# The start of an expert stage: clears and a diagonal moved to other engines, the first gather split in two

## What is computed

```python
h = modulate(rmsnorm(x, norm_g[i, 1]), sh2, sc2)
x = x + g2[:, None, :] * hier_moe(h, ...)        # 32 experts, 2 of them for each token

p_top, g_sel = lax.top_k(p_group, 1)             # one of 4 groups of 8 experts
e_val, e_sel = lax.top_k(fine, TOP_E)            # two experts in the group
gate = p_top * softmax(e_val)
y = (silu(x_rows @ w_gate[e]) * (x_rows @ w_up[e])) @ w_down[e]   # 1024 -> 512 -> 1024
out = zeros.at[row_token].add(y * row_gate)
```

## Time and profile before

| | us |
|---|---|
| median of 3 runs | 2112.96 (2109.74 to 2113.27) |
| the profiled execution | 2108.52 |
| its span in the profile | 2106.8 |
| PE busy | 2007.1 (95%) |
| DVE busy | 907.2 (43%) |
| ACT busy | 364.6 (17%) |
| POOL busy | 90.4 (4%) |
| transfers | 592.65 MB, mean 281 GB/s |

### The profile page before, as it was taken

One profiled execution on the slowest core, in us unless ns is written; L12 is line 12 of the kernel. 1 busy time (PEld: TensorE's weight loads), 2 busy tenths in 40 slices (PEclk: granted clock), 3 DMA queues, 4 the chain that ended last, 5 costly groups with the idle time before them and its releaser, 6 DMA issues.

```text
span 2106.8 us, 21679 instructions
## 1 busy us (share of the span) xinstructions
PE 2007.1 (95%) x8126; PEld 1108.9 (53%) x8126; DVE 907.2 (43%) x1851; ACT 364.6 (17%) x747; POOL 90.4 (4%) x179
## 2 busy tenths in 40 slices
PE   8989999998999999799999999989999999999997
PEld 5556666555766658454444344447765444344442
DVE  3354562335355337776676666752444011000102
ACT  2321000032100010121111111112332111111110
POOL 1121110011111000000000000000000000000000
PEclk9999999999999999999999999999999999999999
DMA  7337885232588641539999999973252999999995
GB/s 274 125 109 255 304 321 202 105 131 109 209 320 301 251 167 40 203 152 406 422 420 427 422 422 420 422 259 120 80 200 81 409 427 423 420 415 421 419 417 222
DMA packets 109524, 592.65 MB, mean 281 GB/s; under 512 B 16663, under 2 KB 21270, under 8 KB 84886
## 3 DMA queue, kind: packets, MB, share of 16 engines
q1 hardware_dynamic: 96406, 541.48, 64.0%
q0 software_dynamic: 13056, 50.33, 6.3%
HBM read 590.74 MB, written 1.05 MB: 281 GB/s over the span
## 4 chain that ended last, share of the span: by engine, by line
PE 89%; DVE 4%; DMA 2%; ACT 2%; issue 1%; POOL 1%; SPq 0%; POOLq 0%; DVEq 0%; ACTq 0%
PE bank L1091 31%; PE bank L752 11%; PE bank L765 10%; PE bank L976 6%; PE bank L688 6%; PE bank L1082 5%; PE bank L1077 5%; PE bank L889 3%; PE bank L996 2%; DMA ring<-in_moe_w_up 2%; PE bank L800 1%; PE bank L1207 1%; ACT work L1571 1%; PE bank L1225 1%; PE bank L1116 1%
## 5 line engine op out<-in xcount | busy, mean ns | idle before, releaser
L1091 PE MATMUL bank<-ring,work 128*64 128x512 f32 x3072 | 677.0, 595 | 29.1 <-ACT work L1571 27.8
L1091 PEld LDWEIGHTS bank<-ring,work 128*64 128x64 f32 x3072 | 229.8, 137 | 444.6 <-issue 444.0
L2378 DVE SCALAR_TENSOR_TENSOR work<-work 128x512 f32<-128x512 f32 x384 | 258.6, 745 | 5.1 <-DVE work L2375 4.9
L752 PE MATMUL bank<-hT,ring 128*128 128x256 f32 x1024 | 223.4, 379 | 0.7 <-ACT hT L1365 0.7
L765 PE MATMUL bank<-ring,work 128*128 128x512 f32 x512 | 222.5, 592 | 0.0
L752 PEld LDWEIGHTS bank<-hT,ring 128*128 128x128 f32 x1024 | 194.4, 190 | 32.6 <-issue 6.9
L2382 DVE SCALAR_TENSOR_TENSOR work<-work,bank 128x512 f32<-128x512 f32 x32 | 22.0, 688 | 428.6 <-ACT work L1559 428.6
L2100 DVE SCALAR_TENSOR_TENSOR work<-ring,cond,work 128x512 f32<-128x512 f32 x168 | 126.3, 752 | 105.6 <-DMA ring<-in_ada_w 100.4
L765 PEld LDWEIGHTS bank<-ring,work 128*128 128x128 f32 x512 | 97.2, 190 | 115.6 <-issue 114.8
L976 PE MATMUL bank<-hT,ring 128*128 128x256 f32 x608 | 137.5, 388 | 0.5 <-ACT hT L1479 0.5
L688 PE MATMUL bank<-ring,hT 128*128 128x512 f32 (+1 forms) x320 | 135.0, 579 | 0.0
(11 more groups left out here) (384 smaller groups left out, 1514.3 us busy)
## 6 DMA issues: line engine op xcount, KB each, us to landing
ring<-in_moe_w_gate SPq DMA_DIRECT2D x64, 2048.0 KB, 13.3
ring<-in_moe_w_up SPq DMA_DIRECT2D x64, 2048.0 KB, 16.4
ring<-in_moe_w_down SPq DMA_DIRECT2D x64, 2048.0 KB, 12.3
ring<-in_ada_w POOLq DMA_DIRECT2D x48, 1024.0 KB, 9.5
ring<-in_w_up SPq DMA_DIRECT2D x16, 2048.0 KB, 13.1
ring<-in_w_down SPq DMA_DIRECT2D x16, 2048.0 KB, 10.0
ring<-in_w_in SPq DMA_DIRECT2D x10, 2048.0 KB, 7.8
ring<-in_cd_w_in SPq DMA_DIRECT2D x6, 2048.0 KB, 9.3
```

What stands on the lines that cost most here:

```text
L752: last = pe.matmul(B(4 + b)[:, (c % 2) * S:(c % 2) * S + S], w[:, k, c * P:c * P + P], hT[:, k, :], start=(k == 0), stop=(k == DT - 1))
L1091: last = pe.matmul(b[h, :], x[:, k, h], w[e][:, k, c0:c0 + 512], start=(k == 0), stop=(k == kk - 1))
L2378: mo.do(dve.scalar_tensor_tensor(fl(bias[:, h]), mask_b, rbt[:, bass.ds(12 * bk + h, 1)], fl(bias[:, h]), ALU.mult, ALU.add))
```

## The change

It does these things at once.

- Entry: POOL clears `zeros`, `pgT` and `ye` behind the root of the second row, and ACT builds `dg_m` behind its copies. DVE copies out its share of the transposed tokens ahead of the second row's squares (`between`). `first_hot` does two dependent operations as one for each row. PE does all four clears before it waits for the selection; the pass count gets a bank and a count of its own.
- The first gather is `gather_pair(0)`, for two experts, 128 columns instead of 256. The other two experts' gather, `gather_pair(1)`, stands between the down halves of the first pair. The first quad is written out for this, and the loop runs over the six in the middle. The counts of `gathered` and `xt_drained` are renumbered (`XT_PASS`).
- In every pair `hidden` waits for the first down half's drain ahead of the gate product, and for the second half's ahead of the up product.
- DVE's bias sums are dealt out anew: a whole bucket ahead of the next `pick`, a whole one behind it, one less after the quad.
- Exit: the first scatter waits for the halves one by one, `updated` works by halves in both rows, and the first row's squares go to ACT (`first_squares`).

The diff, cut to this; indentation is reduced and empty lines are left out:

```diff
@@ -649,6 +650,12 @@
 for n, (cols, width) in enumerate(STATS2):
     power2(n, cols, width)
+    if n in (NORM_STAT[1] + 1, NORM_STAT[3] + 1):
+        own.do(pool.memset(zeros, 0.0))
+        own.do(pool.memset(pgT, 0.0))
+        own.do(pool.memset(ye, 0.0))
+        own.wait()
+        pool.sem_inc(sM["zero_ready"], 1)
...
@@ -1052,13 +1059,14 @@
     pe.wait_ge(m["zero_ready"], i + 1)
     clear((3,))
+    pe.wait_ge(m["exp_in"], 2 * i + 1)
+    clear((0, 1, 2))
     pe.wait_ge(m["sel_ready"], i + 1)
     pe.matmul(B(5)[:, 0:NE], earlier[:, :], sel_e[:, 0, :], start=True, stop=True)
     pe.matmul(B(5)[:, NE:2 * NE], ones[:, :], sel_e[:, 0, :], start=True, stop=False)
-    pe.matmul(B(5)[:, NE:2 * NE], earlier[:, :], sel_e[:, 1, :], start=False, stop=True)
-    pe.matmul(B(5)[:, 2 * NE:3 * NE], ones[:, :], sel_e[:, 0, :], start=True, stop=False)
-    pe.matmul(B(5)[:, 2 * NE:3 * NE], ones[:, :], sel_e[:, 1, :], start=False, stop=True).then_inc(m["rank_ps"], 1)
-    clear((0, 1, 2))
+    pe.matmul(B(5)[:, NE:2 * NE], earlier[:, :], sel_e[:, 1, :], start=False, stop=True).then_inc(m["rank_ps"], 1)
+    pe.matmul(B(4)[:, 0:NE], ones[:, :], sel_e[:, 0, :], start=True, stop=False)
+    pe.matmul(B(4)[:, 0:NE], ones[:, :], sel_e[:, 1, :], start=False, stop=True).then_inc(m["rank_ps"], 1)
...
@@ -1077,11 +1085,24 @@
                 last = pe.matmul(b[:, (d % 2) * S:(d % 2) * S + S], xn[:, t, d * P:d * P + P], pick[:, t, :], start=(t == 0), stop=(t == TT - 1))
         last.then_inc(m["gathered"], 1)
-    def scatter(t, ends=False):
+    def gather_pair(j, xt, banks):
+        for piece, b in enumerate(banks):
+            if piece >= 2 and j == 1:
+                pe.wait_ge(m["xt_drained"], xt + piece - 1)
+            for d in (2 * piece, 2 * piece + 1):
+                for t in range(TT):
+                    last = pe.matmul(b[:, (d % 2) * P:(d % 2) * P + P], xn[:, t, d * P:d * P + P], pick[:, t, P * j:P * j + P],
+                                     start=(t == 0), stop=(t == TT - 1))
+            last.then_inc(m["gathered"], 1)
+    def scatter(t, ends=False, drained=None):
         for hf in range(2):
+            if drained is not None:
+                drained(hf)
...
@@ -1091,17 +1112,17 @@
             last = pe.matmul(b[h, :], x[:, k, h], w[e][:, k, c0:c0 + 512], start=(k == 0), stop=(k == kk - 1))
         return last
-    def hidden(it, j):
+    def hidden(it, j, xt):
         pr = 2 * it + j
         x = xeT[:, :, P * j:P * j + P]
-        pe.wait_ge(m["y_drained"], 2 * pr + 2)
         for b, c, name in ((G, 0, "g_filled"), (U, 1, "u_filled")):
+            pe.wait_ge(m["y_drained"], 2 * pr + 1 + c)
             pe.wait_ge(landedM[c], 16 * pr + 16)
             pe.wait_ge(landedM[c + 3], 16 * pr + 16)
             for k in range(DT):
-                if c == 0 and j == 0 and k % 2 == 0:
-                    pe.wait_ge(m["xt_drained"], 4 * it + 1 + k // 2)
+                if c == 0 and k % 2 == 0:
+                    pe.wait_ge(m["xt_drained"], xt + 1 + k // 2)
                 last = product(b, x, (wslot[c], wslot[c + 3]), k, DT, 0)
             last.then_inc(m[name], 1)
...
@@ -1138,14 +1159,18 @@
                 pe.wait_ge(m["pickg_ready"], it + 1)
             gates_turned(it, j)
             down(pr, 0)
+            if first and j == 0:
+                pe.wait_ge(m["pg_drained"], pr + 2)
+                gather_pair(1, xt + 4, (X, T, X, T))
             if more and j == 1:
+                done = xt + (8 if first else 4)
                 pe.wait_ge(m["p_ready"], it + 2 + i)
                 pe.wait_ge(m["pg_drained"], pr + 2)
                 gather(0, X)
                 gather(1, T)
-                pe.wait_ge(m["xt_drained"], 4 * it + 5)
+                pe.wait_ge(m["xt_drained"], done + 1)
                 gather(2, X)
-                pe.wait_ge(m["xt_drained"], 4 * it + 6)
+                pe.wait_ge(m["xt_drained"], done + 2)
                 gather(3, T)
             down(pr, 1)
...
@@ -1154,14 +1179,14 @@
         pe.wait_ge(m["p_ready"], it0 + 1 + i)
         pe.wait_ge(s2["xn_scaled"], i + 1)
         pe.wait_ge(m["y_drained"], 2 * PAIRS * (q + before) + 2)
-        for piece, b in enumerate((G, U, X, T)):
-            gather(piece, b)
-        with pe.Fori(0, QUADS - 1) as qd:
-            quad((q + before) * QUADS + qd, True)
-        quad((q + before) * QUADS + QUADS - 1, False)
+        xt0 = (q + before) * XT_PASS
+        gather_pair(0, xt0, (G, U, X, T))
+        quad(it0, xt0, True, True)
+        with pe.Fori(1, QUADS - 1) as qd:
+            quad((q + before) * QUADS + qd, (q + before) * XT_PASS + 4 + 4 * qd, True)
+        quad((q + before) * QUADS + QUADS - 1, xt0 + 4 * QUADS, False)
     pe.wait_ge(m["pg_drained"], PAIRS * (n + before) + 1)
-    pe.wait_ge(m["y_drained"], 2 * PAIRS * (n + before) + 2)
-    scatter(0, True)
+    scatter(0, True, lambda hf: pe.wait_ge(m["y_drained"], 2 * PAIRS * (n + before) + 1 + hf))
     scatter(1, True)
...
@@ -1530,6 +1555,9 @@
 def moe(i, before):
     m = sM
     raw_drains(i)
+    for d in range(DT):
+        ins = act.activation(dg_m[:, d, :], ident[:, :], ACT.Copy, scale=modc[:, i, 40 + d:41 + d])
...
             gate(pr)
             hidden_turned(pr)
             gates_turned(pr)
             down(pr, 0)
+            if first and j == 0:
+                gathered_pair(xt + 4, 1, (X, T, X, T))
             if more and j == 1:
...
-                    gathered(it + 1, piece, b)
+                    gathered(xt + (8 if first else 4), piece, b, xeT, S)
             down(pr, 1)
...
-            gathered((q + before) * QUADS, piece, b)
-        with act.Fori(0, QUADS - 1) as qd:
...
+        xt0 = (q + before) * XT_PASS
+        gathered_pair(xt0, 0, (G, U, X, T))
+        quad((q + before) * QUADS, xt0, True, True)
+        with act.Fori(1, QUADS - 1) as qd:
+            quad((q + before) * QUADS + qd, (q + before) * XT_PASS + 4 + 4 * qd, True)
+        quad((q + before) * QUADS + QUADS - 1, xt0 + 4 * QUADS, False)
     return n
+def first_squares(i):
+    k = NORM_STAT[2 * i + 2]
...
 n0 = moe(0, 0)
+first_squares(0)
 scaled_first(2)
...
@@ -1828,36 +1871,37 @@
         wait()
         ins.then_inc(s2["xT_dve"], 1)
-def updated(n, filled, scratch, after):
+def updated(n, filled, scratch, after, between=None, act_squares=False):
     r = []
-    filled(0, 1)
-    do(dve.tensor_tensor(scratch[0], both(0), gbc2, ALU.mult))
-    wait()
-    dve.tensor_tensor(xres[:, 0, :], xres[:, 0, :], scratch[0], ALU.add).then_inc(s2["x_half"], 1)
-    dve.wait_ge(s2["x_half"], n)
-    r.append(squared(0, scratch[0]))
-    for hf in range(2):
-        c = slice(512 * hf, 512 * hf + 512)
-        filled(1, hf)
-        do(dve.tensor_tensor(scratch[1][:, c], B(2 + hf), gbc2[:, c], ALU.mult))
+    for t in range(TT):
+        done = s2["x_half" if t == 0 else "x_done"]
+        halves = [slice(0, 512), slice(512, 1024)] if t == 1 or act_squares else [slice(0, 1024)]
+        for hf, c in enumerate(halves):
+            filled(t, hf if len(halves) == 2 else 1)
+            do(dve.tensor_tensor(scratch[t][:, c], both(t)[:, c], gbc2[:, c], ALU.mult))
+            wait()
+            ins = dve.tensor_tensor(xres[:, t, c], xres[:, t, c], scratch[t][:, c], ALU.add)
+            if hf < len(halves) - 1:
+                do(ins)
         wait()
-        ins = dve.tensor_tensor(xres[:, 1, c], xres[:, 1, c], scratch[1][:, c], ALU.add)
-        if hf == 0:
-            do(ins)
-    wait()
-    ins.then_inc(s2["x_done"], 1)
-    dve.wait_ge(s2["x_done"], n)
-    r.append(squared(1, scratch[1]))
+        ins.then_inc(done, 1)
+        dve.wait_ge(done, n)
+        if t == 1 and between is not None:
+            between()
+        r.append(squared(t, None if t == 0 and act_squares else scratch[t]))
     after(r)
 def squared(t, scratch):
     k = n_stat[0]
     n_stat[0] += 1
-    dve.tensor_tensor_reduce(scratch, xres[:, t, :], xres[:, t, :], 1.0, 0.0, ALU.mult, ALU.add,
-                             stat[:, k % len(STATS), 0:1]).then_inc(s2["stat_ready"], 1)
-    dve.wait_ge(s2["stat_ready"], k + 1)
+    if scratch is not None:
+        if k > 0:
+            dve.wait_ge(s2["stat_ready"], k)
+        dve.tensor_tensor_reduce(scratch, xres[:, t, :], xres[:, t, :], 1.0, 0.0, ALU.mult, ALU.add,
+                                 stat[:, k % len(STATS), 0:1]).then_inc(s2["stat_ready"], 1)
+        dve.wait_ge(s2["stat_ready"], k + 1)
     def root():
         dve.wait_ge(s2["rstd_ready"], k + 1)
...
 def first_hot(dst, vals, top, n, m, how=ALU.is_equal):
-    do(dve.tensor_tensor(fk[:, :, 0:n], vals, spread(top, 2, n), ALU.is_equal))
-    wait()
-    do(dve.tensor_tensor(fk[:, :, 0:n], fk[:, :, 0:n], desc[:, :, 0:n], ALU.mult))
+    for t in range(TT):
+        do(dve.scalar_tensor_tensor(fk[:, t, 0:n], vals[:, t, :], top[:, t:t + 1], desc[:, t, 0:n], ALU.is_equal, ALU.mult))
     wait()
     do(dve.tensor_reduce(rsm[:, 20:22], fk[:, :, 0:n], AX_X, ALU.max))
...
```

(22 more changed lines are left out.)

42 lines of the change are left out of this document (24 added, 18 removed).

## The result

The changed kernel takes 2095.07 us (median, 2090.99 to 2095.66); the kernel before took 2112.81 beside it. The ratio is 0.9918, 95% interval 0.9903 to 0.9933. On a second chip it was 0.9943 (0.9929 to 0.9957), a gain of 12.0 us. The forecast of 2090 was too low by a fifth of the gain: 22.6 us were promised, 17.8 came, and on the second chip about half.

A forecast was written before the change was run, and what follows sets the result against it. The prediction held that transfers would bind the expert stages after the change, slightly above TensorE's need. Entry -10.2, stages -5.7 and exits -6.7 sum to -22.6 us: 2090 us against the 2112.96 median, range 2081 to 2101.

The forecast's parts named there:

- TensorE as the bound: Rival for the expert stages: every quad takes TensorE's 57.85 us, total -38, 2075 us; chance 8 in 100.
- The quad forecast: Expert stages: transfers set each quad's time, 58.6 us if always fed, 59.1 with dips.
- 0.5 us a quad: Expert stages: allowance for the queue running dry, 0 to 1.3, below today's 1.3 because down loads are issued earlier.
- The rival of staying dips: Expert stages: dips belong to the queue itself, quads stay at 59.94, total -12.7, 2100 us; chance 20 in 100.
- The split gather: Entry: first gather at 128 columns takes 3.7 us instead of 7.07, -3.4; its second half costs 4.1 in the first pair.
- the down loads' start: First pairs of a stage: both down loads, issued to a queue just run dry, need 12.65 us.
- the stage's -2.1 and -3.65: First and second expert stage: each falls to 467.4 us, from 469.5 and 471.05, -5.7 together.
- Clears and routing: Entry: earlier clears and shorter routing start the gather at 1608.5 instead of 1611.74, -3.2 us in each stage.
- the term of 1.5 (0 to 3): Entry: half clock for most of the first gather, after TensorE stands some 2.5 us, costs +1.5 us a stage.
- The exit: Stage exits: earlier start and work by halves give -4.2 us after the first stage, -2.5 at the end.
- The first stage's masked sums: First stage: DVE's sums of a second bucket (8.04 us) move ahead of the second gate product at cost 0.
- The slower rival: Expert stages: an entirely bound queue runs dry each quad; at 61.5 us a quad +6, 2119 us; chance 4 in 100.

The follow-up runs named there:

- e11: Changed kernel loading only half of each up matrix from a stage's second pair on, the product using what stood in the slot: 2067.25 us in one run.
- e9: Changed kernel with the whole first gather ahead of the first pair and each later quad's gather behind the second down half: 2082.58 us, ratio to before 0.9876.
- e6: Changed kernel with the first gather made for all four experts at once again, ahead of the first pair: ratio to before 0.9929.
- e8: The changed kernel itself, unedited, run again on a second chip: ratio to before 0.9943.
- e1: Kernel before with only the split wait (first down half's drain ahead of gate, second's ahead of up) added: ratio to before 0.9936, 13.5 us faster.
- e4: Changed kernel with each down load issued as two column halves, the first after the first down half: 2109.55 us, ratio to before 1.0006.
- e5: Changed kernel with the second half of the first gather moved behind the first pair's second down half: ratio to before 0.9938.
- e12: Changed kernel, first gather still split, with its second half and every later gather behind the second down half of their pair: 2083.75 us, ratio to before 0.9886.
- e3: Changed kernel with three more zero products on TensorE between the ranking and the first gather: ratio to before 0.9919.

## Why the prediction was right, and where not

**The bound.** That a quad would be set by the transfers was right, and TensorE as the bound (2075) was rightly put low: only e11, with bytes left out, shows it. The quad forecast, 59.1, came out at 59.03 and 59.42. TensorE's quad was read as 59.70 less the waits in brackets, 57.85; it is 57.40. So two waits of 0.93 on average in brackets cost 1.15 each. The time for TensorE as the bound would be 5 us lower (an estimate, 0.45 in each of 12 quads).

The rate of a fed queue was read well: 430 GB/s in the earlier trace rows against 428.5 measured over a quad. Against this, the Trainium skill, "DMA: Bandwidth & Descriptors", section Anatomy of one DMA, has 436 for the moving part. It has it for transfers that GpSimd issues, while SyncE issues these loads. No stretch of 60 us here reached it, and e9, never dry, shows 429: an estimate of 57.7 us a quad by the page's figure stays 1 us below what was measured.

**The dips.** (A dip is the time for which the queue runs dry.) 0.5 us a quad was right: it was 0.4 in the first stage (59.03 - 58.6) and 0.8 in the second, where some 0.25 of the 0.8 is not a dip but a fall of the clock (see the sum). The reason given, that a faster TensorE asks for down loads sooner, was half of it: with the gather ahead of the last down half they still came too late in some quads, and e9 shows the dips gone once it stands behind. The rival of staying dips (2100) was wrong in saying that the dips belong to the queue itself.

**The split gather** is the step that the text had wrong, though it did not spoil the sum. The entry was booked with -3.4 for it, plus 1.5 for the clock. In the stage its second half stood as 4.1 us ahead of the issue at 62.0, and then the text said that it "costs nothing beyond the down loads' start, as TensorE waits for the queue later anyway". That start is all there is to it: every later load hangs on it. The sum did hold the 4.1 (62.0 came out exactly, 1666.36 - 1604.4), but the text never set it against the 3.4 of the entry. Without the split the same working gives 57.9 for 62.0 and a stage of 463.3, 4.1 less, against an entry 3.4 longer and some more for the clock: nothing won by splitting. e6 against e8 bears that out. So the stage's -2.1 and -3.65 were not the worth of the split wait but what was left of it: e1 has 3.6 and 5.1.

**The entry.** Clears and routing: gather 9.25 us after the router's last product instead of 12.34, -3.1 for the forecast -3.2. No cover failed: the gate row starts right behind the router at 1588.58, and neither ACT's diagonal nor POOL's memsets are waited for. The half gather took 5.18 in the first stage, 5.2 by forecast, and 6.62 in the second, where the clock was at its lower level throughout: the term of 1.5 (0 to 3) was 1.5 and 2.9, and the second is where the entries fell short. The Trainium skill, "TensorE: Matmul & The Clock Gate", Part 1, would have had the clears keep the clock through the ranking. The trace agrees as far as that (0.98 in 1594 to 1597), and then it fell in the 2.5 us of standing ahead of the gather.

**The exit.** 10.2 us for the forecast 9.8, and 14.3 at the end: -3.9 and -2.7 for -4.2 and -2.5.

**The first stage's masked sums** cost nothing, as forecast. TensorE's waits in 919 to 1388, all that the view has:

```profile
PE bank L1112 <- DMA ring<-in_moe_w_up: 10.0, 7, 1.9
```

**The sum.** Forecast 22.6; measured in the span 17.8. Short are the stages by 3.3 (5.7 against 2.4) and the entries by 1.3 (10.2 against 8.9). The stages' share has two parts. The first is the down loads' start, the term mis-sized. The first wait for a load ended 95.3 us into each stage (1699.73 - 1604.38), not at 94.25: 1.0 late, twice. A down issue to a queue that has just run dry was costed at 12.65 for both loads, read at 1044.14. But there the last up load landed 2 us after that issue (asked for at 1026.0, 20.2 to landing), so the queue had hardly stopped. In the changed kernel the last up load landed only 0.7 us after the issue at 62.0, and both down loads took 13.7 (the second was issued some 0.45 behind 1666.36 and landed 13.2 later). The working also has two slips of 0.1 or less (62.0 + 12.65 is 74.65, and 25.17 MB at 430 GB/s are 58.5 us), which change nothing.

The second part is one that I had no term for: at one of the waits for up loads in the second stage the clock fell, and the product behind it took 8.79 us instead of 7.09 (1759.66 above). The next such wait ended 60.19 us later, the one after that 58.73, so the fall cost some 1.5 us. Without it the steady quads lost 0.4 and some 0.6 us, close to the forecast 0.5. The slower rival, a dip of over 2.4 us in each quad, did not come. e4 shows another way to lose it all.

## What to carry to other kernels

When a stretch is bound by a queue whose issues hang on the progress of an engine, what counts is the engine's time to each issue, not its total. Work taken out of the entry and put ahead of such an issue is not saved. Work moved behind the issue is saved where no later issue becomes the late one: here 4 to 8 us a stage for the later quads' gathers (e9), and nothing for the half gather (e5, e12), which was given back at the next issue. So for each term moved into a stage, look for the next issue behind it and set the delay against what the move saves, and go on to the issue after that one.

## What the runs showed of the hardware

- TensorE's clock can fall in the middle of a dense stage. In the changed kernel TensorE had worked without a gap (1754 to 1757), stood 2.30 us for a load, and then the granted clock was at its lower level for part of the product that it had waited to do:

```profile
1754.00:1757.00 3.00, 3.00 (x16) 0.87 (x12) 0.00 (x0) 0.00 (x0) 0.00 (x0) 1.00 1.01 431
...
1759.00:1762.00 3.00, 2.34 (x8) 0.88 (x10) 0.00 (x0) 0.00 (x0) 0.00 (x0) 0.78 1.01 431
1762.00:1765.00 3.00, 3.00 (x12) 1.26 (x10) 0.00 (x0) 0.00 (x0) 0.00 (x0) 0.65 1.00 426
```

  It cost 1.7 us. The traces of e1 and e3 to e8 each show one to four such products (8.4 to 8.8 us), behind waits of 1.96 to 2.76 us; other waits as long cost nothing (e1 had 2.70 at 1825.70, and the product took 7.09). In e9 and e12, whose waits are 0.2 to 1.4 us, there is none. In which of the waits the clock falls, no run explains. So a late load costs its wait and sometimes up to 1.7 us more. That is likely part of why e9 gained more than expected; no run separates it.
- The size of a row of a transfer still tells at 2 KB. The queue's packets went from 96,406 to 154,774 with the down loads in column halves (a third of the bytes), and the same 60 us moved 413 GB/s instead of 428. With the gate loads in 8 KB rows (105,622 packets) no loss can be read.
- A wait of 0.9 us in brackets between two groups of products cost TensorE 1.15 us, by the quads of e11 and of before (59.70 - 57.40 for two). e9 agrees: its one wait of 1.11 us a quad makes it 1.33 longer than e11's.
